# Projections of the first head in another order; GLU inputs split inside the first block, the last head's norm between GLU tiles

## The reference, cut to what matters

```
h = rmsnorm(x); q, k, v, gate, u = split(h @ w_in)
y_ret = silu(gate) * head_groupnorm(retention(rope(q), rope(k), v)) * gain     # 4 heads of 128
y_ssm = gelu(s5_scan(u, ...))                                                 # 4 tiles of 128 channels
glu_a, glu_b = split(y_ssm @ w_glu);  y_ssm = glu_a * sigmoid(glu_b)
mix = concat(y_ret, y_ssm) @ w_out
x = x + rmsnorm(mix)
```

## Time and profile before

| | us |
|---|---|
| runs | 3067.21, 3057.79, 3064.99 |
| median | 3064.99 |
| profiled execution, its own time | 3058.22 |
| span of its profile | 3056.4 |
| PE busy in the span | 2826.0 (92%) |
| DVE, ACT, POOL busy | 1607.4, 614.9, 957.3 |

### The profile page before, as it was taken

The page is one execution under the profiler, slowest core; times in us unless marked ns, Lnnn a source line. Parts: engine busy times, 40 slices in busy tenths (PEclk is TensorE's granted clock), DMA queues, the critical chain, the costliest instruction groups (busy, mean ns, idle before and its releaser), DMA issues. The chain is left out here.

```text
span 3056.4 us, 33833 instructions
## 1 busy us (share of the span) xinstructions
PE 2826.0 (92%) x13246; PEld 2299.6 (75%) x13246; DVE 1607.4 (53%) x2052; ACT 614.9 (20%) x985; POOL 957.3 (31%) x515
## 2 busy tenths in 40 slices
PE   6899969999999999987896998889999999999997
PEld 5788857887788777866784776557887788888885
DVE  8776424745544445475655895664256422222247
ACT  3323232311100011122221003543112100111101
POOL 2122204453333323441121332001354533333343
PEclk9999989999999999987897999999999999999998
DMA  3111132332212222221010343113133211111123
GB/s 126 39 49 55 46 138 76 104 104 97 89 55 75 84 87 84 81 97 58 21 35 28 97 121 105 71 42 152 56 103 97 79 46 52 47 47 47 46 69 103
DMA packets 88630, 229.83 MB, mean 75 GB/s; under 512 B 27536, under 2 KB 30608, under 8 KB 88528
## 3 DMA queue, kind: packets, MB, share of 16 engines
q1 hardware_dynamic: 52528, 173.72, 17.5%
q10 hardware_dynamic: 36000, 54.69, 5.5%
HBM read 197.84 MB, written 29.36 MB: 74 GB/s over the span
## 5 line engine op out<-in xcount | busy, mean ns | idle before, releaser
L195 POOL CAST w_hi<-w_raw 128x1024 fp32r<-128x1024 f32 x254 | 282.3, 1112 | 2037.5 <-PE ps L208 2026.1
L204 PE MATMUL ps<-a_hi,w_hi 128*128 128x512 f32 x2080 | 696.9, 401 | 44.7 <-PEq L2649 18.8
L206 PE MATMUL ps<-a_lo,w_hi 128*128 128x512 f32 x2080 | 682.5, 394 | 0.0
L208 PE MATMUL ps<-a_hi,w_lo 128*128 128x512 f32 x2080 | 681.4, 393 | 0.0
L197 POOL TENSOR_TENSOR w_lo<-w_raw,w_hi 128x1024 fp32r<-128x1024 f32 x254 | 671.9, 2645 | 20.3
L204 PEld LDWEIGHTS ps<-a_hi,w_hi 128*128 128x128 f32 x2080 | 392.7, 191 | 130.4 <-issue 29.2
L208 PEld LDWEIGHTS ps<-a_hi,w_lo 128*128 128x128 f32 x2080 | 395.5, 190 | 84.8
L206 PEld LDWEIGHTS ps<-a_lo,w_hi 128*128 128x128 f32 x2080 | 396.4, 191 | 83.4
L206 PE MATMUL ps<-g_b,w_hi 128*128 128x512 f32 x1216 | 413.3, 396 | 0.0
L204 PE MATMUL ps<-g_b,w_hi 128*128 128x512 f32 x1088 | 364.9, 398 | 39.5 <-DVE g_b L1326 19.4
L208 PE MATMUL ps<-g_b,w_lo 128*128 128x512 f32 x1088 | 361.2, 394 | 0.0
(11 more groups left out here) (406 smaller groups left out, 3014.1 us busy)
## 6 DMA issues: line engine op xcount, KB each, us to landing
w_raw<-in_wstream SPq DMA_DIRECT2D x254, 512.0 KB, 3.5
ada_w<-in_ada_w ACTq DMA_DIRECT2D x24, 512.0 KB, 3.6
ada_w_m<-in_ada_w ACTq DMA_DIRECT2D x24, 512.0 KB, 4.3
y_by_token<-y ACTq DMA_DIRECT2D x12, 512.0 KB, 2.6
tmp_b<-mixer_out SPq DMA_DIRECT2D x8, 512.0 KB, 3.3
x_res_b<-in_xT SPq DMA_DIRECT2D x2, 2048.0 KB, 12.3
x_block<-x_res_b SPq DMA_DIRECT2D x16, 256.0 KB, 3.1
z_rows<-ada_w ACTq DMA_DIRECT2D x8, 512.0 KB, 2.7
```

Source lines behind the costliest of these rows:

```text
L195: pool.tensor_copy(k.w_hi[:, s, :], k.w_raw[:, s, :]).then_inc(k.w_high, 1)
L204: pe.matmul(o, w_hi, a_hi[:, c], start=first, stop=False)
L206: pe.matmul(o, w_hi, a_lo[:, c], start=False, stop=False)
L208: ins = pe.matmul(o, w_lo, a_hi[:, c], start=False, stop=last)
```

## The change

In head 0, PE runs V whole after K and before the state transposes; Q takes V's place around U_GROUPS. DVE runs rotations(0), V's scaling, kernel_rows(0), angles(1) and only then states(0). ACT swaps the halves of K before it evacuates the state matrices, and runs parameters_act(1) right after the mT transfers, ahead of Q's halves.

At the end of block 1, when the last projection tile is done, SP loads the stored ssm results of heads 0 to 2 into y_raw, which lies on a_lo (dead by then), then weight tiles 22 and 23, then the retention results of heads 0 to 2, and waits for these. ACT and DVE split the ssm tiles in block 1; that of head 3 is split straight from PSUM and never stored. Of head 3 only the retention products are done in block 1. raw, swap, vT and yc get addresses that block 2 doesn't overwrite early.

In block 2, retention tiles 0 to 2 are split from y_raw, GLU is written out tile by tile, the sigmoid waits for the first half of its tile (`b_done`), and centred, variance and spread of head 3 stand behind GLU tiles 0, 1 and 2. GLU's outputs go to w.g_hi, w.g_lo, and `output_halves_pe` takes its two halves from two places, with the wait for the GLU outputs between the halves of its first tile.

```diff
         def _(sp):
-            stream_load(sp, k, 2, P1_TILES + 4)
+            stream_load(sp, k, 2, P1_TILES + 2)
+            sp.wait_ge(k.tile_done, P1_TILES)
+            sp.wait_ge(ssm_out, 16 * (HEADS - 1))
+            for i in range(HEADS - 1):
+                sp.dma_start(y_raw[HEADS + i][:, :], d.y_scr[HEADS + i, :, :]).then_inc(ssm_in[i], 16)
+            stream_load(sp, k, P1_TILES + 2, P1_TILES + 4)
+            sp.wait_ge(ret_out, 16 * (HEADS - 1))
+            for i in range(HEADS - 1):
+                sp.dma_start(y_raw[i][:, :], d.y_scr[i, :, :]).then_inc(ret_in, 16)
+            sp.wait_ge(ret_in, 16 * (HEADS - 1))
...
         def _(pe):
-                    tile_half(0, K_, 0)
-                    tile_half(0, K_, 1)
+                    for t in (K_, V_):
+                        tile_half(0, t, 0)
+                        tile_half(0, t, 1)
...
-                tile_half(i, V_, 0)
+                tile_half(i, V_ if i else Q_, 0)
...
-                tile_half(i, V_, 1)
+                tile_half(i, V_ if i else Q_, 1)
...
-                tile_half(i, Q_, 0)
-                tile_half(i, Q_, 1)
+                if i:
+                    tile_half(i, Q_, 0)
+                    tile_half(i, Q_, 1)
...
             retention(HEADS - 1)
-            centred(HEADS - 1)
-            variance(HEADS - 1)
-            spread(HEADS - 1)
...
         def _(act):
+                    halves_swapped(0, K_, 1)
+                    parameters_in(1)
                     state_transposed(0)
-                halves_swapped(i, K_, 1)
...
+                if i == 0:
+                    parameters_act(1)
                 act.wait_ge(kT_ready, i + 1)
                 halves_swapped(i, Q_, 2)
...
+            high(0)
+            high(1)
+            job(HEADS - 1, SSM_T)
+            act.activation(k.a_hi[:, 2 * HEADS - 1, :].rearrange("p (n t) -> p t n", t=STEP),
+                           Xf[region(HEADS - 1, SSM_T)].rearrange("p (t n) -> p t n", n=NBLK), ACT.Copy).then_inc(ssm_high, 1)
             retention(HEADS - 1)
-            centred(HEADS - 1)
-            deviation(HEADS - 1)
-            retention_out(HEADS - 1)
-            act.wait_ge(ssm_out, 16 * HEADS)
-            act.wait_ge(ret_out, 16 * HEADS)
+            high(2)
...
         def _(dve):
                     rope(0, K_, 1, kT, kT_ready)
+                    rotations(0)
+                    projected(0, V_, vT)
                     kernel_rows(0)
-                    rotations(0)
+                    angles(1)
...
                 states(i)
-                if i == 0:
-                    angles(1)
-                elif following:
+                if i and following:
                     state_inputs(i + 1)
...
     def tensor(pe):
+        between = (centred, variance, spread, None)
+        for i in range(GLU_TILES):
+            q = i % 2
+            pe.wait_ge(k.w_split, base + i + 1)
+            pe.wait_ge(s["b_free"], i)
+            tile_products(pe, k, q, g_hi, g_lo, [(X[0][:, h, :], half_of(h)) for h in range(2)], kts=HEADS)\
+                .then_inc(s["b_done"], 1)
+            pe.wait_ge(k.pair_free[q], base // 2 + i // 2)
+            tile_products(pe, k, q, g_hi, g_lo, both_halves(k, q), kts=HEADS, at=HEADS * P).then_inc(k.tile_done, 1)
+            if between[i]:
+                between[i]()
         pe.wait_ge(s["mlo"], HEADS)
-        pe.wait_ge(s["ylo"], HEADS)
-        output_halves_pe(pe, k, turn, out0, w.a_hi, w.a_lo)
+        output_halves_pe(pe, k, turn, out0, [(w.a_hi, w.a_lo, 0), (w.g_hi, w.g_lo, 0)],
+                         lambda: pe.wait_ge(s["ylo"], GLU_TILES))
```

More of the change, by code:

```diff
@@ L1280, in tensor, with centred @@
     def tensor(pe):
[L1281 to L1291, removed]
+        def centred():
+            for h in range(2):
+                ins = pe.matmul(X[1][:, h, :], k.mats[:, CENTER, :], raw[:, half_of(h)], start=True, stop=True)
+            ins.then_inc(s["centre"], 1)
@@ new lines, in variance, with spread @@
+        def variance():
+            pe.wait_ge(s["centred"], 1)
+            for c in range(NC):
+                ins = pe.matmul(Xf[1][:, c:c + 1], sq[:, c * P:(c + 1) * P], k.head_col[:, :], start=True, stop=True)
+            ins.then_inc(s["variance"], 1)
+        def spread():
+            pe.wait_ge(s["inv"], 1)
+            for c in range(NC):
+                ins = pe.matmul(Xf[1][:, c * P:(c + 1) * P], rcol[:, c:c + 1].broadcast_to([P, P]), k.mats[:, IDENT, :],
+                                start=True, stop=True)
+            ins.then_inc(s["row"], 1)
@@ L1303, in scalar, with high @@
[L1303 to L1311, removed]
+        def high(t):
+            act.activation(w.a_hi[:, t, :], ret[t][:, :], ACT.Copy).then_inc(s["mhi"], 1)
@@ new lines, in gated, with out @@
+        def gated(i):
+            act.wait_ge(s["b_done"], i + 1)
+            if i:
+                act.wait_ge(k.pair_free[(i - 1) % 2], base // 2 + (i - 1) // 2 + 1)
+            act.activation(w.acc[:, :], Xf[0], ACT.Sigmoid).then_inc(s["b_free"], 1)
+        def out(i):
+            q = i % 2
+            act.wait_ge(k.pair_free[q], base // 2 + i // 2 + 1)
+            act.activation(w.g_hi[:, i, :], w.mix[:, q, :], ACT.Copy).then_inc(s["yhi"], 1)
+        for t in range(LAST):
+            high(t)
@@ L1322, in vector, with low, glu @@
         tt = dve.tensor_tensor
[L1323 to L1336, removed]
[L1337 to L1339 removed]
+        def low(t):
+            dve.wait_ge(s["mhi"], t + 1)
+            tt(w.a_lo[:, t, :], ret[t][:, :], w.a_hi[:, t, :].bitcast(F32), ALU.subtract).then_inc(s["mlo"], 1)
+        def glu(i):
+            q = i % 2
+            dve.wait_ge(s["b_free"], i + 1)
+            dve.wait_ge(k.tile_done, base + i + 1)
+            if i >= 2:
+                dve.wait_ge(s["ylo"], i - 1)
+            tt(w.mix[:, q, :], pair[q], w.acc[:, :], ALU.mult).then_inc(k.pair_free[q], 1)
+            dve.wait_ge(s["yhi"], i + 1)
+            tt(w.g_lo[:, i, :], w.mix[:, q, :], w.g_hi[:, i, :].bitcast(F32), ALU.subtract).then_inc(s["ylo"], 1)
+        for t in range(LAST):
+            low(t)
+        glu(0)
+        glu(1)
+        dve.wait_ge(s["root"], 1)
+        dve.reciprocal(rcol[:, :], col[:, :]).then_inc(s["inv"], 1)
+        glu(2)
+        dve.wait_ge(s["row"], 1)
+        gain = VEC["gn"][0] + LAST
+        dve.scalar_tensor_tensor(out=yc[:, :], in0=yc[:, :], scalar=k.vecs[:, gain:gain + 1], in1=Xf[1], op0=ALU.mult,
+                                 op1=ALU.mult).then_inc(s["normed"], 1)
+        dve.wait_ge(s["normed"], 1)
+        tt(ret[LAST][:, :], yc[:, :], gate[:, :], ALU.mult).then_inc(s["retained"], 1)
+        low(LAST)
+        glu(3)
         output_halves_dve(dve, turn, lambda m, h: None)
```

100 lines of the change are left out of this document (64 added, 36 removed).

## The result

| | before | after |
|---|---|---|
| median of six runs | 3066.09 | 3045.39 |
| lowest and highest | 3057.79, 3071.08 | 3040.63, 3047.46 |
| profiled execution, span | 3056.4 | 3040.5 |

The ratio is 0.9933, 95% interval 0.9918 to 0.9947: 20.7 us faster, 16 to 25 by the interval. The forecast was 3035.0 with a range of 3022 to 3045; the sign was right, the time lies 10.4 us above the forecast and 0.4 us above the range.

The account below looks back on a forecast made before the run. PE was taken as the busy engine over most of the span, with waits at the seam and in the first head. Seam -29.8 plus head +3.6 gave -26.2 us: 3032.0 to 3038.8, forecast 3035, range 3022 to 3045.

Parts of the forecast that it names:

- the three waits: PE's waits up to 560 us: 19.4 us for the first GLU tile, 9.7 ahead of SCORES, 4.7 ahead of K_ROWS.
- the mechanism of the seam: Between blocks 1 and 2: norm chain, DRAM write, eight loads and splits leave the path; gain 29.8 us, bounds 25 and 32.
- the norm's blocks: Three small PE blocks of the norm between GLU tiles, taken as 5.7 us together; one in earlier heads took 1.95 us.
- PE's wait for the last subtraction: First output tile after GLU: PE waits 2 us until multiply, copy and subtract of GLU tile 3 end near 450.
- PE's new wait: Between the halves of the first output tile, for the GLU outputs: PE reaches it at 448.8.
- A: First head: the 4.7 us wait goes and SCORES comes earlier by that much; total -34.5 us, 3023.7; chance 0.18.
- C: GLU and beyond: PE's clock stays at the lower level, turning -26 into +26, 3084; chance 0.02.
- B: Seam gives less: loads hold SP's last wait or the norm's chain runs late; priced 8 us, 3040; chance 0.12.
- Behind it the work is the same and PE-bound.: Everything behind the seam, from the first output tile on: claimed unchanged and bound by PE, with no further term.
- the level: Starting time: profiled execution 3058.22 becomes 3032.0, the median's level gives up to 3038.8; 3035 was put between.
- the worst of the head: First head: SCORES at 124.9 instead of 121.29, a 3.6 us loss, at worst a loss of 6.
- a half-missed seam: Range's upper end: the seam's gain of 29.8 us falling half of the way to its lower bound of 25.

Follow-up runs that it names:

- seam_only: The changed kernel without its new order in head 0, which runs as in the kernel before: median 3036.93 us, ratio 0.9904.
- head_only: The kernel before with only the new order in head 0: median 3067.93 us, ratio 1.0009.
- loads_and_stores: seam_only with two stores put back on ACT's queue and two loads on SP's, as many transfers as in the kernel before: 3036.54 us in one run.
- second pair of profiles: Both kernels unchanged, profiled and timed again: the kernel before 3068.93 us in one run, the changed kernel median 3044.01 us.
- x_late_add: The kernel before with the second mixer's first x_block load waiting for DVE's last sum of squares: matmuls 7000 to 7250 took 82.6 us.

## Why the prediction was right or wrong

**Right.** The reading of the three waits, and the mechanism of the seam: the six loads never held anybody up, the block ended with low(2), GLU ran without waits, the norm's blocks took 1.88 and 1.84 us, PE's wait for the last subtraction 2.0 us for 2. With the head's 3.3 us taken off, GLU started at 393.4 (forecast 393.9). At the first output tile the seam alone had given 29.8 us, the figure of the forecast (28.1 by seam_only against before, 30.0 by after against head_only). That it is the same to 0.1 us is luck. From the first GLU matmul to PE's new wait took 53.5 us (396.73 to 450.24), where the sum had 54.9, and the start was 0.5 us early. Against that, the sum put the second half of the first output tile at full clock, 2.7 us, though the old tile started low; it took 4.45 us (452.29 to 456.74), with a granted clock of 0.50 from 453 to 455. In loads_and_stores, where the clock stayed at 1.00 there, the first output tile (matmuls 1152 to 1176, PE's wait included) took 7.81 us instead of 9.38. In the head: 3.1 us of idle PE at U_GROUPS for 3, SCORES at 124.77 for 124.9. Rivals A and C fell; B's 3040 is nearer to the time than the forecast is, but its mechanism didn't occur.

**Wrong: "Behind it the work is the same and PE-bound."** The work is the same; PE-bound it is not everywhere. At the residual in the second mixer PE already waited 2.7 us for DVE, which waited for a DMA, and a row of the page of before would have shown it. The sum had no term for what lies behind the first output tile. In the chain that ended last of before the load stands with DVE's residual:

```profile
PE ps L204 9%; PE ps L206 9%; PE ps L208 9%; DMA mix_b<-z_rows 1%; DMA x_res_b<-x_block 1%; DVE x_res_b L1101 1%; DVE mix_b L1098 1%; DVE a_lo L1112 0%; DVE g_b L1630 0%; PE ps L1033 0%; DVE tmp_b L1626 0%; DVE tmp_b L1124 0%; DVE acc_b L1082 0%; PE ps L1019 0%; DVE mix_b L2635 0%
```

A landing 0.8 us later cost 2.2 to 2.9 us there.

**Wrong: the level.** The sum was made against 3058.22, which is the lower end of what the kernel before does, and the forecast was put between that level and the median's. Against the median of six runs, 3066.09, the same -26.2 gives 3039.9. This is the largest single part.

**What the 10.4 us are:** 4.9 the level; -1.0 because up to matmul 1500 the gain was 27.2 us, not 26.2 (the output tiles' 1.2 us below within it; in the second pair of profiles it was 25.7, so this term is itself scatter); 2.7 the residual of the second mixer; the remaining 3.8 I can't tell from the scatter, for the ratio's interval is some 4.5 us wide to either side: the first three lead to 3041.6, and the interval is 3041 to 3050. The range ended at 3045 because it took the worst of the head and a half-missed seam above the median's level (by its own terms 3038.8 + 2.4 + 2.4, which is 3043.6), but had no term for anything behind the first output tile.

## What to carry to other kernels

When work moves in the first sixth of a kernel, look in the rest of the trace for the waits that already end with a DMA, or with an engine whose instructions lengthen beside another's: their price can change by more than the shift, and a sum that stops at the edit has no term for them. Make the sum against the median of many runs, and measure the scatter of the stretches that the change doesn't touch before a difference in them is put down to it. A wait on one large transfer of which only the first part is needed at once is worth cutting, with a semaphore for each part: here 6.5 us in the stretch of two such loads, where the whole change gives 20.7.

## What the runs showed of the hardware that I had not expected

- The same instructions on a busy PE take 78.3, 81.5 or 83.8 us in one stretch of 250 large matmuls (1500 to 1750), with the clock at its lower level for 3.4, 10.2 or 15.3 us of it; in one place 7 us hold 52 matmuls at a granted clock of 1.00 and 38 at 0.76. Two profiles of the kernel before differ in it.
- One 2 MB load lands in 10.6 to 11.0 us in the kernels with the old seam (11.5 in x_late_add) and in 11.6 to 12.2 with the new one, issued at the same place beside the same weight loads. The number of earlier transfers on its queue or on SP's doesn't decide it. One 16 KB packet of kind "instruction", about 1 us long, falls before the load in the first and into it in the second; a 512 KB weight load that it falls into lands in 4.8 to 4.9 us, else in 3.5 to 3.6.
- In the output tiles of block 1 the mean spacing of large matmuls rose from 227 to 231 ns at full clock (5.44 to 5.53 us a tile), in every kernel with the new seam and to the nanosecond alike, 1.2 us in all. Half of the operands have new places, but matmuls of either half are slower (231 and 230 ns in after). Its cause is open and was not tried.
- A DVE instruction with two inputs in SBUF that meets POOL's subtraction can last until POOL is done, or some tenths longer, whatever its size: 2.32 us for 16 columns (else 0.17), 2.13 for 512 (else 0.69), 2.70 for 508 (else 0.69). Those with one input in PSUM are not held up: in before, inside a subtraction from 2258.51 to 2261.25, two of 512 columns took 0.67 and 0.73 us, and 0.67 to 0.75 elsewhere.
